# Transposes in pieces of 7, 3, 4 and 2, turned groups finished by halves, and the squares of x taken from its transposed copy

## The reference

```
h    = rms_norm(x, norm_mix_g);  proj = h @ w_in          # q, k, v of retention and attention
ret  = silu(gate) * group_norm(retention(rq, rk, rv))
att  = sliding_window_attention(aq, ak, av, sinks)        # 32 heads, 4 key heads, chunks of 64
x    = x + (sigmoid(h @ w_gate) * [ret @ w_ret, att @ w_att]) summed @ w_out
h2   = rms_norm(x, norm_ffn_g)
x    = x + square(relu(h2 @ w_up)) @ w_down               # width 8192
out  = rms_norm(x, norm_final_g)
```

## Time and profile before

| | us |
|---|---|
| three runs: lowest, median, highest | 1511.77, 1512.82, 1512.90 |
| the profiled execution, its own time | 1512.22 |
| its span, from the first to the last instruction | 1510.3 |
| PE busy in the span | 1495.5 (99%) |
| DVE busy | 1025.1 (68%) |
| ACT busy | 791.1 (52%) |

### The profile page before, as it was taken

One profiled execution on the slowest core, in us unless ns is written; L12 is line 12 of the kernel. 1 busy time (PEld: TensorE's weight loads), 2 busy tenths in 40 slices (PEclk: granted clock), 3 DMA queues, 4 the chain that ended last, 5 costly groups with the idle time before them and its releaser, 6 DMA issues.

```text
span 1510.3 us, 18941 instructions
## 1 busy us (share of the span) xinstructions
PE 1495.5 (99%) x7008; PEld 1285.5 (85%) x7008; DVE 1025.1 (68%) x1360; ACT 791.1 (52%) x1023; POOL 39.3 (3%) x52
## 2 busy tenths in 40 slices
PE   9999999999999999999999999999999999999998
PEld 7788888888888888888888888888888888888886
DVE  5987987555556777777799877338753586438745
ACT  6555555444444454444444555556555555555553
POOL 0000000000000000000000000000000000000000
PEclk9999999999999999999999999999999999999999
DMA  9644545666655665565765888898888878888783
GB/s 362 209 159 167 188 148 174 207 202 225 220 182 184 197 210 170 192 216 195 248 224 193 249 232 275 250 261 233 232 279 249 255 233 253 257 250 254 230 263 116
DMA packets 154392, 333.93 MB, mean 221 GB/s; under 512 B 5600, under 2 KB 5728, under 8 KB 149856
## 3 DMA queue, kind: packets, MB, share of 16 engines
q1 hardware_dynamic: 149296, 299.61, 58.3%
q0 software_dynamic: 4464, 32.51, 11.6%
q10 hardware_dynamic: 576, 1.06, 0.2%
HBM read 298.55 MB, written 2.10 MB: 199 GB/s over the span
## 4 chain that ended last, share of the span: by engine, by line
PE 81%; DVE 12%; issue 3%; DMA 2%; ACT 1%; SPq 0%; POOL 0%; POOLq 0%; DVEq 0%; ACTq 0%
PE acc L437 78%; DVE buf L1004 6%; DVE wlo L995 3%; DMA raw<-in_w_in 2%; DVE buf L1382 1%; ACT buf L686 1%; PE tps L452 1%; PE pps L479 1%; PE pps L462 0%; DVE kT L1004 0%; DVE qT L1004 0%; PE sps L470 0%; DVE ta_lo L1410 0%; PE tps L580 0%; PE tps L582 0%
## 5 line engine op out<-in xcount | busy, mean ns | idle before, releaser
L672 ACT ACTIVATE whi<-raw 128x1024 fp32r<-128x1024 f32 x542 | 568.8, 1055 | 558.1 <-PE acc L437 553.1
L995 DVE TENSOR_TENSOR wlo<-raw,whi 128x1024 fp32r<-128x1024 f32 x480 | 584.2, 1225 | 367.5 <-ACT whi L672 363.4
L437 PE MATMUL acc<-whi,ta_hi 128*128 128x512 f32 x1308 | 502.7, 384 | 4.3 <-DVE wlo L995 3.8
L437 PE MATMUL acc<-whi,ta_lo 128*128 128x512 f32 x1308 | 495.7, 379 | 0.0
L437 PE MATMUL acc<-wlo,ta_hi 128*128 128x512 f32 x1180 | 447.2, 379 | 0.0
L437 PEld LDWEIGHTS acc<-whi,ta_hi 128*128 128x128 f32 x1308 | 247.1, 189 | 52.3 <-DVE wlo L995 11.0
L437 PE MATMUL acc<-whi,tb_hi 128*128 128x512 f32 x736 | 280.1, 381 | 1.0 <-DVE wlo L995 0.7
L437 PE MATMUL acc<-whi,tb_lo 128*128 128x512 f32 x736 | 278.9, 379 | 0.0
L437 PEld LDWEIGHTS acc<-whi,ta_lo 128*128 128x128 f32 x1308 | 247.2, 189 | 35.1
L437 PEld LDWEIGHTS acc<-wlo,ta_hi 128*128 128x128 f32 x1180 | 223.1, 189 | 30.1 <-issue 0.3
L437 PE MATMUL acc<-wlo,tb_hi 128*128 128x512 f32 x616 | 233.5, 379 | 0.0
(11 more groups left out here) (139 smaller groups left out, 792.1 us busy)
## 6 DMA issues: line engine op xcount, KB each, us to landing
raw<-in_w_in SPq DMA_DIRECT2D x66, 1024.0 KB, 5.2
raw<-in_w_up SPq DMA_DIRECT2D x64, 1024.0 KB, 5.8
raw<-in_w_down SPq DMA_DIRECT2D x64, 1024.0 KB, 6.1
raw<-in_w_gate SPq DMA_DIRECT2D x32, 1024.0 KB, 5.4
low<-raw POOLq DMA_DIRECT2D x31, 1024.0 KB, 8.1
raw<-in_w_att SPq DMA_DIRECT2D x16, 1024.0 KB, 5.0
raw<-in_w_ret SPq DMA_DIRECT2D x16, 1024.0 KB, 5.0
raw<-in_w_out SPq DMA_DIRECT2D x16, 1024.0 KB, 5.2
```

Of the source, the lines that this page charges most:

```text
L437: last = nc.tensor.matmul(paired(acc[B.parity][:, t, :]), a[:, k, tok], halves_in_turn(b), start=(k == 0 and n == 0), stop=(k == KCH - 1 a ...
L672: nc.scalar.activation(whi[:, s:s + UCH, :], raw[:, u * UCH:(u + 1) * UCH, :], ACT.Copy).then_inc(hi_ready, 1)
L995: V_.tensor_tensor(wlo[:, s:s + UCH, :], raw[:, u * UCH:(u + 1) * UCH, :], whi[:, s:s + UCH, :].bitcast(f32), ALU.subtract).then_inc(lo_re ...
```

## The change

Four edits.

1. `turn_among`, which serves blocks 33 to 37 and the up blocks of stage 6, puts 7, 3 and 4 transposes ahead of the splits of u3, u4 and u5 and 2 behind them, in place of 8, 4, 2 and 2.
2. A turned group is rounded on ACT and subtracted on DVE by halves, and where PE waits for a fourth group it waits for the first half before u6 and for the second before u7 (new semaphore `first_half`). This holds for all groups of stages 3 to 6.
3. The plain copy `xin` is not loaded. ACT squares the transposed copy `xt` in two halves of 128x2048 into `xsq`, DVE adds the eight slices of each half in pairs (1024, 512 and 256 columns) into `sq_sums`, and PE sums over the partitions with four small float32 matmuls against a column block of ones, between A's u2 and u3; DVE reads the result from `sps`.
4. With it, the order at the start of block A changes: ACT and DVE do two splits, then square or add, then the next split.

```
-            for s in range(2):
-                load(Block(1), w_in[s * 512:(s + 1) * 512, OFF_AQ:OFF_AQ + COLS], s)
-            sp.dma_start(xin[:], x.rearrange("(t p) n -> p t n", p=P)).then_inc(x_full, 16)
...
+            load_block(Block(1), w_in, OFF_AQ)
...
@@ PE, stage 1
-                    gemm(A, ta_hi, ta_lo, 0, 8)
+                    gemm(A, ta_hi, ta_lo, 0, 3)
+                    pe.wait_ge(sq_added, 2)
+                    for t in range(TILES):
+                        for h in range(2):
+                            last = nc.tensor.matmul(sps[:, t, 0:CHUNK], sq_sums[:, h, t * P:(t + 1) * P], ones,
+                                                    start=(h == 0), stop=(h == 1))
+                    last.then_inc(sq_full, 1)
+                    gemm(A, ta_hi, ta_lo, 3, 8)
...
@@ PE, stage 6 (alike in the first blocks of stages 4, 5 and 6)
                     gemm(B[i], hi, lo, 0, 6)
                     if i == 4:
+                        pe.wait_ge(first_half, q * 4 + (T_STAGE6 + 4))
+                    gemm(B[i], hi, lo, 6, 7)
+                    if i == 4:
                         pe.wait_ge(t_free, q * 4 + (T_STAGE6 + 4))
-                    gemm(B[i], hi, lo, 6, 8)
+                    gemm(B[i], hi, lo, 7, 8)
...
@@ ACT
+            def hi_by_halves(src, dst, g):
+                for h in range(2):
+                    nc.scalar.activation(dst[:, ds(g * GCH + h * UCH, UCH), :], src[:, h * UCH:(h + 1) * UCH, :],
+                                         ACT.Copy).then_inc(t_hi, 1)
...
-                    split(A, 0, 4)
-                    act.wait_ge(x_full, 16)
-                    for t in range(TILES):
-                        if t:
-                            act.wait_ge(ssq_ready, t)
-                        nc.scalar.activation(junk[:], xin[:, t, :], ACT.Square, accum_out=ssq[:, t:t + 1]).then_inc(ssq_ready, 1)
-                        split(A, 4 + t, 5 + t)
+                    split(A, 0, 2)
+                    for h in range(2):
+                        half = slice(h * (KCH // 2), (h + 1) * (KCH // 2))
+                        nc.scalar.activation(xsq[:, half, :], xt[:, half, :], ACT.Square).then_inc(squared, 1)
+                        split(A, 2 + h, 3 + h)
+                    split(A, 4, 6)
...
@@ DVE
-                for u, n0, n1 in ((3, 0, 8), (4, 8, 12), (5, 12, 14)):
+                for u, n0, n1 in ((3, 0, 7), (4, 7, 10), (5, 10, 14)):
...
+            def lo_by_halves(n, src, hi, lo, g, done):
+                for h in range(2):
+                    at = ds(g * GCH + h * UCH, UCH)
+                    dve.wait_ge(t_hi, n * 2 + (h - 1))
+                    V_.tensor_tensor(lo[:, at, :], src[:, h * UCH:(h + 1) * UCH, :], hi[:, at, :].bitcast(f32),
+                                     ALU.subtract).then_inc((first_half, done)[h], 1)
...
-                    split(A, 0, 5)
-                    dve.wait_ge(ssq_ready, 2)
-                    V_.tensor_scalar(msq[:, 0:2], ssq[:], 1.0 / D, EPS, ALU.mult, ALU.add).then_inc(ms_ready, 1)
+                    split(A, 0, 2)
+                    for h in range(2):
+                        half = slice(h * (KCH // 2), (h + 1) * (KCH // 2))
+                        dve.wait_ge(squared, h + 1)
+                        for n in (4, 2):
+                            lower, upper = [xsq[:, half.start + i * n:half.start + (i + 1) * n, :] for i in range(2)]
+                            mine.step(V_.tensor_tensor(lower, lower, upper, ALU.add))
+                            mine.wait(dve)
+                        V_.tensor_tensor(sq_sums[:, h, :], xsq[:, half.start, :], xsq[:, half.start + 1, :],
+                                         ALU.add).then_inc(sq_added, 1)
+                        split(A, 2 + h, 3 + h)
+                    split(A, 4, 5)
+                    dve.wait_ge(sq_full, 1)
+                    V_.tensor_scalar(msq[:, 0:2], sps[:, 0:TILES, 0], 1.0 / D, EPS, ALU.mult, ALU.add).then_inc(ms_ready, 1)
```

More of the change, by code:

```diff
@@ L176, in build @@
         nsink = place("nsink", [P, 16], f32)
-        ssq = place("ssq", [P, 2], f32)
         msq = place("msq", [P, 4], f32)
@@ L196, in build @@
         assert here[0] <= nc.sbuf_usable_end, here[0]
-        xin = place("xin", [P, TILES, D], f32, at_b)
+        xsq = place("xsq", [P, KCH, S], f32, at_b)
         xt = place("xt", [P, KCH, S], f32, at_b + 16 * K)
-        junk = place("junk", [P, D], f32, at_c + 24 * K)
         qkT = place("qkT", [P, 2 * RET_HEADS, S], f32, at_c)
@@ L228, in build @@
         xt_full = [sem(f"xt_full{u}") for u in range(UNITS)]
-        first_full, second_full, third_full, x_full = sem("first_full"), sem("second_full"), sem("third_full"), sem("x_full")
+        first_full, second_full, third_full = sem("first_full"), sem("second_full"), sem("third_full")
         xt_gained, xt_hi = sem("xt_gained"), sem("xt_hi")
@@ L240, in build @@
         ret_full, ret_read = sem("ret_full"), sem("ret_read")
-        t_hi = sem("t_hi")
+        t_hi, first_half = sem("t_hi"), sem("first_half")
         hT_ready, retT_ready, h2T_ready = sem("hT_ready"), sem("retT_ready"), sem("h2T_ready")
         own = sem("own")
-        mhalf_set, ssq_ready, ms_ready = sem("mhalf_set"), sem("ssq_ready"), sem("ms_ready")
+        mhalf_set, ms_ready = sem("mhalf_set"), sem("ms_ready")
+        squared, sq_added, sq_full = sem("squared"), sem("sq_added"), sem("sq_full")
         pow_ready, rstd_ready = sem("pow_ready"), sem("rstd_ready")
@@ L277, in build @@
         gained = buf[2][:, 1, :].rearrange("p (k n) -> p k n", n=S)
+        ones = buf[3][:, 0, 0:CHUNK]
+        sq_sums = buf[3][:, 1, :].rearrange("p (h n) -> p h n", n=S)
         gmix_at = slice(SMALL - 4 * KCH, SMALL - 3 * KCH)
@@ L350, in _ @@
             sp.wait_ge(unit_done, 1)
-            for s in range(2):
-                load(Block(1), w_in[s * 512:(s + 1) * 512, OFF_AQ:OFF_AQ + COLS], s)
-            sp.dma_start(xin[:], x.rearrange("(t p) n -> p t n", p=P)).then_inc(x_full, 16)
-            for s in range(2, LOADS):
-                load(Block(1), w_in[s * 512:(s + 1) * 512, OFF_AQ:OFF_AQ + COLS], s)
+            load_block(Block(1), w_in, OFF_AQ)
             load_block(Block(2), w_in, OFF_RQK)
@@ L595, in stage4 @@
                     gemm(Block(B4 + 1), tb_hi, tb_lo, 0, 6)
+                    pe.wait_ge(first_half, 4)
+                    gemm(Block(B4 + 1), tb_hi, tb_lo, 6, 7)
                     pe.wait_ge(retT_ready, 4)
-                    gemm(Block(B4 + 1), tb_hi, tb_lo, 6, 8)
+                    gemm(Block(B4 + 1), tb_hi, tb_lo, 7, 8)
                 else:
@@ L610, in _ @@
                 if j == 0:
+                    pe.wait_ge(first_half, T_STAGE4 + 4)
+                gemm(Block(B5 + j), tc_hi, tc_lo, 6, 7)
+                if j == 0:
                     pe.wait_ge(t_free, T_STAGE4 + 4)
-                gemm(Block(B5 + j), tc_hi, tc_lo, 6, 8)
+                gemm(Block(B5 + j), tc_hi, tc_lo, 7, 8)
             def stage6(q, first, last=False):
@@ L619, in stage6 @@
                     gemm(B[0], ta_hi, ta_lo, 0, 6)
+                    pe.wait_ge(first_half, T_STAGE5 + 4)
+                    gemm(B[0], ta_hi, ta_lo, 6, 7)
                     pe.wait_ge(h2T_ready, 4)
-                    gemm(B[0], ta_hi, ta_lo, 6, 8)
+                    gemm(B[0], ta_hi, ta_lo, 7, 8)
                 else:
@@ L687, in scaled @@
                 return last
+            def hi_by_halves(src, dst, g):
+                for h in range(2):
+                    nc.scalar.activation(dst[:, ds(g * GCH + h * UCH, UCH), :], src[:, h * UCH:(h + 1) * UCH, :],
+                                         ACT.Copy).then_inc(t_hi, 1)
             def hi_from_turned(turn, dst, g):
                 act.wait_ge(t_full, turn + 1)
-                nc.scalar.activation(dst[:, ds(g * GCH, GCH), :], turned, ACT.Copy).then_inc(t_hi, 1)
+                hi_by_halves(turned, dst, g)
             def hi_from_gained(turn, src, dst, g):
                 act.wait_ge(t_free, turn + 1)
-                nc.scalar.activation(dst[:, ds(g * GCH, GCH), :], src[:].rearrange("p t (k n) -> p (t k) n", n=S),
-                                     ACT.Copy).then_inc(t_hi, 1)
+                hi_by_halves(src[:].rearrange("p t (k n) -> p (t k) n", n=S), dst, g)
             def exps(g, c):
@@ L1043, in gain @@
                 V_.tensor_tensor(dst[:].rearrange("p t (k n) -> p (t k) n", n=S), turned, gsl, ALU.mult).then_inc(t_free, 1)
+            def lo_by_halves(n, src, hi, lo, g, done):
[4 more added lines that the diff above has]
+                                     ALU.subtract).then_inc((first_half, done)[h], 1)
             def lo_from_gained(n, src, hi, lo, g, done):
-                dve.wait_ge(t_hi, n)
-                V_.tensor_tensor(lo[:, ds(g * GCH, GCH), :], src[:].rearrange("p t (k n) -> p (t k) n", n=S),
-                                 hi[:, ds(g * GCH, GCH), :].bitcast(f32), ALU.subtract).then_inc(done, 1)
```

(6 more changed lines are left out.)

## The result

The changed kernel takes 1502.21 us (median of 4 runs, 1501.84 to 1502.45) against 1512.40 us (4 runs): ratio 0.9933, interval 0.9915 to 0.995. That is 10.2 us less; 10.1 were forecast. The time itself was forecast as 1502.7 us. It came out 0.5 us lower, mostly because the three runs before had put the old median at 1512.82 us, where four put it at 1512.40. The profiled execution took 1502.11 us, its span is 1500.1 us; before they were 1512.22 and 1510.3.

The account below looks back on a forecast made before the run. PE was taken as the bound, with stalls from late `wlo`, turned groups and DVE's start. Stage 6's 8.3, blocks 33 and 37's 1.25 and the start's 0.6 made 10.1 us won: 1502.7 us, range 1500.9 to 1506.

Parts of the forecast that it names:

- What bounds the kernel: PE stalls: 8.88 us over pure matmuls in stage 6, 1.39 us in blocks 33 and 37, plus the start.
- Edit 1: Stage 6's 16 stalled blocks: u3 and u4 stalls go, u5 becomes late, 0.6 us in all (nothing to 2.6).
- Edit 2: Turned groups: first half ready 0.97 us sooner, u6 stalls go; stage 6 wins 8.3 us; halves' extra time costed at nothing.
- Blocks 33 and 37: Waits at u6 shrink: 0.54 us won in block 33, all 0.71 us in block 37, together 1.25 us.
- Edits 3 and 4: Start up to R's u5: `msq` at about 37.25 us instead of 37.84, 0.6 us won (0.2 to 0.7).
- u5 taking over in full: Stage 6: pieces end 0.13 us later than summed, 16 blocks pay at u5; 8.1 us won, 1504.7; chance 0.17.
- the start losing: Block A: squares and additions delay splits, PE stalls at u3, `msq` 0.9 us later; 8.6 us won, 1504.2; chance 0.08.
- loads becoming the bound: Stage 6: a faster PE would wait for loads, all but the start's gain lost; 1511 us; chance 0.05.
- the clock: Block A: PE stalls for `sq_added`, its clock falls from 2.4 to 1.2 GHz; 1519 us; chance 0.02.

Follow-up runs that it names:

- the early sum: Changed kernel with the four matmuls of ones between A's u1 and u2, `msq` ahead of u4's split: 1500.41 us; with pieces of 7, 3, 3, 3 too: 1499.73 us.

## Why the prediction was right

- *What bounds the kernel.* The excess of 8.88 + 1.39 us over pure matmuls in the windows was the budget; after the change 0.6 + 0.14 us of it are left. With the start the parts add up to the whole: 8.2 + 1.25 + 0.66 = 10.1 us between the two profiles.
- *Edit 1.* Right in place and size: u3 and u4 have 0.5 us or more in hand, and u5 is what is late next, by 0.08 us in block 46 (0.07 forecast). The residue of the 16 blocks is 0.6 us, as forecast, and lies where the sum had put it: 0.05 to 0.06 us in each of the eight blocks of the first and last round, 0.08 in one block of each of the two middle rounds (46 and 54), nothing in the six others. Their leads in the trace are 0.09 to 0.11, 0.07 and 0.15 to 0.16 us, so 0.15 minus the lead is what each pays. The pieces of 7, 3, 3, 3 and of 7, 3, 5, 1 show that it is u5's lead and nothing else.
- *Edit 2.* Right: no stall at u6 in stage 6, and the fixed cost of the halves is hidden; priced at 0.34 us a group, it is about 0.16. The forecast did not say how the two edits depend on each other. Alone they are worth 5.0 and 2.45 us, and with the squares' 0.7 the sum is 8.2, not 10.2. The other 2.0 us exist only with both, since in five blocks (33, 41, 49, 57 and 65) the stall at u4 is given back at u6 unless the group is halved. Their traces say the same: 0.7 to 0.9 us over pure matmuls in each before, nothing won by the pieces alone, 1.6 us in the five by the halves alone, 3.6 by both. What an edit is worth here depends on which wait is next.
- *Blocks 33 and 37.* 20.86 and 20.72 us, so 0.54 and 0.71 us won, to the hundredth.
- *Edits 3 and 4.* 0.6 us forecast, 0.66 in the profiles, 0.7 in the medians of the squares alone. The mechanism holds; that the pair of profiles agrees to the hundredths is in part luck. The matmuls of ones were between their two bounds, but `msq` starts 1.03 us behind the first of them and not 0.9 (0.78 to 1.3 bounded), so 0.44 us were won from block A's start, and 0.22 came from its earlier start. Nor was the old start a fixed time: it moved with the arrival of `xin`, by 0.5 us between three profiles. That the start hangs on DVE's queue behind `msq` is shown by moving it both ways, 1.8 us down and 2.6 us up, and by work added to PE that costs nothing.
- *Rivals.* u5 taking over in full, the start losing, loads becoming the bound (the DMA share of the four groups is 0.83 to 0.85, and they still run at the pace of clean blocks) and the clock all failed to appear: no clock below 1.00 in any window, and no PE wait for `sq_added`.

## What to carry to other kernels

On an engine that is 99% busy by the profile, cut windows at the starts of equal pieces of work and compare them with a clean piece: the excess is what can be won, and the time from a producer's end to the consumer's due time prices every move of an instruction. Work woven between deadlines should be spread so that every deadline has its margin, the last as well. A piece moved away from ahead of a deadline wins what the deadline was missed by and no more (0.06 us a block with pieces of 7, 3, 3, 3); one moved ahead of a deadline without margin costs its whole length (0.45 us a block with 7, 3, 5, 1). Before adding up edits, ask of each which wait it exposes: two that guard successive waits pay in full only together (1.6 us for the halves alone, nothing for the pieces alone, 3.6 us for both, in the five blocks where the waits follow each other).

## What the runs showed of the hardware

- A weight load released late costs more than the lateness: the second matmul starts 0.37 us behind the producer's end, so that a producer has to end 0.15 us ahead of the due time. It held where the first matmul started 0.05, 0.06, 0.08 and 0.11 us behind the producer's end (u4 before, u5 with 7, 3, 5, 1, u5 in the changed kernel, u3 before, all in block 46). Six blocks of the changed kernel with leads of 0.15 to 0.16 us at u5 pay nothing.
- Four float32 matmuls with 128 rows of weights and 64 moving columns hold PE for 0.80 us (36.15 to 36.95 us), with the reader 1.03 us behind their start. Their busy time is 1.00 us; four with 64 rows have 0.66 us by the same measure (the scores).
- POOL's power (the -1/2 of `rstd`) on 128x2 elements took 0.70 to 0.71 us in the nine traces in which DVE stood idle beside it, and 1.54 us in the two in which DVE ran a split of 128x1024 at the same time (the two with the early sum). `rstd_half` follows `msq` by 1.05 us in the former and 1.89 us in the latter. Why is not shown.
- Two half-width instructions in a row cost less than their sum: 1.29 us on DVE for two of 0.69, 1.15 us on ACT for two of 0.62.
- The start of the second block scatters between 28.07 and 29.00 us over eleven profiled executions, one of each kernel. The waits ahead of it are for the first loads, but what makes them scatter is not shown. A difference of half a microsecond in a kernel of this kind should be read from the distance to such a mark and not from the clock of one profile.
